# One channel tile of a depthwise convolution goes from TensorE to ScalarE and GpSimd

## What is computed

```
def mixer_conformer_conv(x, w_pw1, b_pw1, w_dw, b_dw, ln_g, ln_b, w_pw2):
    h = x @ w_pw1 + b_pw1
    a, g = jnp.split(h, 2, axis=-1)
    h = a * jax.nn.sigmoid(g)
    h = causal_depthwise_conv(h, w_dw) + b_dw          # 31 taps, each channel on its own
    h = jax.nn.silu(layer_norm(h, ln_g, ln_b))
    return h @ w_pw2
```

## Time and profile before

| | |
|---|---|
| median of 3 runs | 2520.3 us (2519.31 to 2522.27) |
| the profiled execution | 2518.05 us, its span 2516.3 us |
| TensorE busy | 2491.3 us, 99% |
| VectorE, ScalarE, GpSimd busy | 1921.5, 1124.3, 2.4 us |
| TensorE's granted clock | 1.0 of full speed over the span |
| TensorE's taps, layer 0 | from 100.3 to about 156.6 us |
| the same, layer 3 | from 1986.7 to about 2044.5 us |

### The profile page before, as it was taken

How to read it: one execution, slowest core, us unless ns; L and a number is a source line. 1 busy time by engine, 2 the same in 40 slices (tenths; PEclk the granted TensorE clock), 3 DMA queues, 4 the chain that set the end, 5 groups by cost and what they waited for, 6 DMA issues and landing times.

```text
span 2516.3 us, 43772 instructions
## 1 busy us (share of the span) xinstructions
PE 2491.3 (99%) x18687; PEld 2281.9 (91%) x18687; DVE 1921.5 (76%) x2564; ACT 1124.3 (45%) x1580; POOL 2.4 (0%) x15
## 2 busy tenths in 40 slices
PE   9999999999999999999999999999999999999999
PEld 7899999889888899998898899998898899999888
DVE  7779999578454689995784479997677779999576
ACT  4466444336233254443362245444353476444335
POOL 0000000000000000000000000000000000000000
PEclk9999999999999999999999999999999999999999
DMA  5203333323222223333233324333223203333322
GB/s 157 69 27 94 104 107 102 108 79 132 99 93 85 90 86 108 103 109 101 84 101 95 98 67 118 110 102 109 92 86 101 67 27 94 107 104 109 102 84 76
DMA packets 264502, 238.15 MB, mean 95 GB/s; under 512 B 14396, under 2 KB 210292, under 8 KB 264180
## 3 DMA queue, kind: packets, MB, share of 16 engines
q1 hardware_dynamic: 263732, 234.84, 30.0%
q10 hardware_dynamic: 576, 0.52, 0.1%
HBM read 233.21 MB, written 2.10 MB: 94 GB/s over the span
## 4 chain that ended last, share of the span: by engine, by line
PE 87%; DVE 4%; ACT 0%; issue 0%; DVEq 0%
PE psum L985 15%; PE psum L1150 10%; PE psum L1152 10%; PE psum L1151 9%; PE psum L853 9%; PE psum L854 9%; PE psum L855 9%; PE psum L871 3%; PE psum L873 3%; PE psum L872 3%; PE psum L843 2%; PE psum L844 2%; PE psum L849 2%; PE psum L914 2%; DVE w_lo L1687 1%; PE psum L1193 1%
## 5 line engine op out<-in xcount | busy, mean ns | idle before, releaser
L1687 DVE TENSOR_TENSOR w_lo<-raw,w_hi 128x1024 fp32r<-128x1024 f32 x287 | 345.3, 1222 | 255.2 <-ACT w_hi L1270 254.7
L1270 ACT CAST w_hi<-raw 128x1024 fp32r<-128x1024 f32 x287 | 295.2, 1046 | 403.7 <-DMA raw<-in_ffn_w_down_dram 101.1
L853 PE MATMUL psum<-h_hi,w_lo 128*128 128x512 f32 x872 | 341.5, 392 | 0.0
L855 PE MATMUL psum<-h_hi,w_hi 128*128 128x512 f32 x872 | 339.4, 389 | 0.0
L854 PE MATMUL psum<-h_lo,w_hi 128*128 128x512 f32 x856 | 333.2, 389 | 0.0
L985 PE MATMUL psum<-a_hi,w_lo 128*128 128x256 f32 x1088 | 275.3, 282 | 6.8 <-DVE w_lo L1687 3.8
L985 PE MATMUL psum<-a_hi,w_hi 128*128 128x256 f32 x1088 | 271.5, 279 | 0.0
L1152 PE MATMUL psum<-h_hi,w_hi 128*128 128x256 f32 x768 | 218.2, 284 | 0.0
L1151 PE MATMUL psum<-h_hi,w_hi 128*128 128x256 f32 x768 | 217.2, 283 | 0.0
L985 PEld LDWEIGHTS psum<-a_hi,w_lo 128*128 128x128 f32 x1088 | 204.4, 188 | 8.9 <-DVE w_lo L1687 3.4
L1282 ACT CAST w_hi<-w_hi_f 128x1024 fp32r<-128x1024 f32 x96 | 101.1, 1053 | 233.0 <-DVE w_hi_f L1715 233.0
(11 more groups left out here) (326 smaller groups left out, 6124.6 us busy)
## 6 DMA issues: line engine op xcount, KB each, us to landing
raw<-in_ffn_w_gate_dram SPq DMA_DIRECT2D x176, 256.0 KB, 3.0
raw<-in_ffn_w_up_dram SPq DMA_DIRECT2D x176, 256.0 KB, 3.4
raw<-in_ffn_w_down_dram SPq DMA_DIRECT2D x176, 256.0 KB, 3.0
raw<-in_a_w_pw_dram SPq DMA_DIRECT2D x94, 256.0 KB, 3.0
raw<-in_ple_w_gate_dram SPq DMA_DIRECT2D x64, 256.0 KB, 3.0
raw<-in_b_w_in_dram SPq DMA_DIRECT2D x64, 256.0 KB, 3.0
raw<-in_c_w_in_dram SPq DMA_DIRECT2D x48, 256.0 KB, 2.9
raw<-in_b_w_out_dram SPq DMA_DIRECT2D x32, 256.0 KB, 3.0
```

The costliest lines, as they stand in the source:

```text
L853: pe.matmul(bank(grp.g, j), st_lo, mv_hi, start=(k == 0), stop=False, skip_group_check=by_tiles(grp))
L855: done = pe.matmul(bank(grp.g, j), st_hi, mv_hi, start=False, stop=(ku == last and a == UK - 1), skip_group_check=by_tiles(grp))
L1270: act.copy(hi_u[u % RING], raw_u[u % RING]).then_inc(hi_ready, 1)
L1687: dve.tensor_tensor(lo_u[u % RING], raw_u[u % RING], hi_u[u % RING].bitcast(F32), ALU.subtract)\
```

## The change

Tile 2 leaves `QUADS`. ScalarE multiplies the shifted `conv_x` by the tap weight, once for each of the 31 taps, into a ring of five buffers of 512 words; GpSimd adds each product to the tile in `h_f32` where the moved segments also lie. ScalarE's products stand behind its weight casts of groups 2 and 3, four for each (`TAPS_UNIT`). Product k from the sixth on waits until the add that frees its buffer is done; each add waits for its product and for the add before it.

The segments are then tiles 3, 4, 5, 6 and the two halves of 7. The rough mean is asked for at step 29 of segment 1 instead of step 14 of segment 3. VectorE waits for the last add in front of `centre_sum`, sums tiles 0, 1 and 2, moves the low half of segment 0 itself and adds tile 3. Moves, centring, sums and squares are regrouped to match; the order of the last statements of the norm's first half changes a little on ScalarE and VectorE.

```diff
-QUADS = (2, 3, 4, 5, 6, 7)
-A_BLOCKS = 5
+POOL_TILE = 2
+PRODUCTS, TAPS_UNIT = 5, 4
+QUADS = (3, 4, 5, 6, 7)
+A_BLOCKS = 4
...
-SEGMENTS = ((0, None), (1, None), (2, None), (3, None), (4, None), (5, 0), (5, 1))
-WHOLE = 5
-CENTRE_IN, CENTRE_AT = 3, 14
+SEGMENTS = ((0, None), (1, None), (2, None), (3, None), (4, 0), (4, 1))
+CENTRE_IN, CENTRE_AT = 1, 29
...
+        def tap_product(k):
+
+            at = A_BLOCKS * BLOCK_WORDS + CW + k % PRODUCTS * SEQ
+            return a_f32[:, at:at + SEQ]
...
+            for s in stages:
+                if s.kind != "conv_in":
+                    continue
+                c, y = s.layer // 3, tiles(h_f32, CONV_Y + POOL_TILE)
+                for k in range(1, TAPS_A):
+                    pool.wait_ge(tap_made, TAPS_A * c + k + 1)
+                    if k > 1:
+                        pool.wait_ge(tap_added, (TAPS_A - 1) * c + k - 1)
+                    pool.tensor_tensor(y, tap_product(k - 1) if k == 1 else y, tap_product(k), ALU.add).then_inc(tap_added, 1)
...
+            def tap_products(s, first, end):
+
+                for k in range(first, min(end, TAPS_A)):
+                    if k >= PRODUCTS:
+                        act.wait_ge(tap_added, (TAPS_A - 1) * (s.layer // 3) + k - PRODUCTS + (k == PRODUCTS))
+                    act.activation(tap_product(k), conv_x[:, POOL_TILE, k:k + SEQ], ACT.Identity,
+                                   scale=col("a_w_dw", s.layer // 3 * TAPS_A + k, POOL_TILE)).then_inc(tap_made, 1)
...
                 half_moments(s, 0)
                 half_root(s, 0)
                 load_silu()
+                half_affine_pair(s, 0, 0)
                 move(s, LAST, 1)
-                half_affine_pair(s, 0, 0)
                 half_affine_pair(s, 0, 1)
...
+                        conv_by_phase(s, 3)
                         conv_by_phase(s, 4)
-                        conv_by_phase(s, 5)
                         split_more(AHEAD)
-                        for i in range(2):
-                            move(s, i, 1)
-                            move(s, i, 0)
-                        move(s, 2, 0)
+                        move(s, 0, 1)
                         save_centre(s)
+                        move(s, 1, 1)
+                        act.wait_ge(moved_low, moved(s, 0))
+                        move(s, 1, 0)
                         conv_squares(s)
-                        act.wait_ge(moved_high, moved(s, 2))
+                        conv_square(s, 4)
+                        move(s, 2, 1)
+                        conv_square(s, 5)
                         move(s, 3, 1)
...
                             split_to(u + 1)
+                            if grp.index == 2 and u == grp.unit + LEAD:
+                                act.wait_ge(prod_ready, s.prod0 + POOL_TILE // 2 + 1)
+                            if grp.index >= 2:
+                                made = (TILES * (grp.index - 2) + u - grp.unit - LEAD) * TAPS_UNIT
+                                tap_products(s, made, made + TAPS_UNIT)
...
             def centre_sum(s):
 
                 own.settle()
+                partial, bias = tiles(tmp, 4), lambda m: conv_bias(s, m)
+                dve.wait_ge(tap_added, (TAPS_A - 1) * (s.layer // 3 + 1))
+                own.add(dve.scalar_tensor_tensor(partial, conv_tile(2), bias(2), conv_tile(0), ALU.add, ALU.add))
+                own.settle()
+                own.add(dve.tensor_tensor(partial, partial, conv_tile(1), ALU.add))
+                move(s, 0, 0)
                 wait_moved(s, 0)
-                wait_moved(s, 1)
-                for m in range(2):
-                    own.add(dve.scalar_tensor_tensor(tiles(tmp, 4 + m), conv_tile(2 + m), conv_bias(s, 2 + m), conv_tile(m),
-                                                     ALU.add, ALU.add))
-                own.settle()
-                dve.tensor_tensor(ysum[:, :], tiles(tmp, 4), tiles(tmp, 5), ALU.add).then_inc(ysum_ready, 1)
+                own.settle()
+                dve.scalar_tensor_tensor(ysum[:, :], conv_tile(3), bias(3), partial, ALU.add, ALU.add).then_inc(ysum_ready, 1)
...
                         make_blocks(s, 4)
-                        make_blocks(s, 5)
                         lo_to(ahead)
```

More of the change, by code:

```diff
@@ L34 @@
 LAST = len(SEGMENTS) - 1
-Z_READY = 3 + len(SEGMENTS) - 2
-SQ_READY = len(SEGMENTS) - 1
+Z_READY = 4 + len(SEGMENTS) - 2
+SQ_READY = len(SEGMENTS)
 SGU_BLOCK = 128
@@ L375, in tap_blocks @@
             return h_f32[:, SPLIT_LOW:SPLIT_LOW + (TAPS_A + 2) * PAIR_ROWS]
+        def tap_product(k):
+            at = A_BLOCKS * BLOCK_WORDS + CW + k % PRODUCTS * SEQ
+            return a_f32[:, at:at + SEQ]
+        assert A_BLOCKS * BLOCK_WORDS + CW + PRODUCTS * SEQ <= 2 * DT * SEQ
         def rows(ap, r):
@@ L573, in trunk @@
         moved_low = sem("moved_low")
+        tap_made = sem("tap_made")
+        tap_added = sem("tap_added")
         proj_sq = sem("proj_sq")
@@ L1350, in conv_half_square @@
                 m, h = QUADS[SEGMENTS[i][0]], SEGMENTS[i][1]
-                act.wait_ge(z_ready, Z_READY * (s.layer // 3) + i + 2)
+                act.wait_ge(z_ready, Z_READY * (s.layer // 3) + i + 3)
                 act.activation(hcol(square(m), h), hcol(tiles(h_f32, CONV_Y + m), h), ACT.Square).then_inc(sq_ready, 1)
@@ L1660, in _ @@
                             split_to(u + 1)
+                            if grp.index == 2 and u == grp.unit + LEAD:
[3 more added lines that the diff above has]
+                                tap_products(s, made, made + TAPS_UNIT)
                             if u == s.groups[3].unit + s.groups[3].units + 1:
-                                for n in range(4):
+                                for n in range(3):
                                     conv_by_phase(s, n)
@@ L1841, in conv_sums_of @@
                 sum_sq, sum_z, both = tiles(tmp, 4), tiles(tmp, 5), tiles(tmp, 4, 2)
-                move(s, 2, 1)
                 dve.wait_ge(centre_saved, c + 1)
@@ L1847, in conv_sums_of @@
                 place_centred(s, 3)
-                wait_moved(s, 2)
-                place_centred(s, 4)
-                move(s, 3, 0)
                 dve.wait_ge(z_ready, z0 + 3)
@@ L1854, in conv_sums_of @@
                 own.add(dve.tensor_tensor(sum_z, sum_sq, sum_z, ALU.add))
-                wait_moved(s, 3)
-                place_centred(s, 5)
+                wait_moved(s, 1)
+                place_centred(s, 4)
+                dve.wait_ge(z_ready, z0 + 4)
+                own.settle()
+                own.add(dve.tensor_tensor(sum_z, sum_z, conv_tile(4), ALU.add))
+                move(s, 2, 0)
                 dve.wait_ge(sq_ready, SQ_READY * c + 1)
                 own.add(dve.tensor_tensor(tiles(tmp, 0, 2), tiles(tmp, 0, 2), tiles(tmp, 2, 2), ALU.add))
[L1859 to L1862, removed]
+                own.settle()
                 own.add(dve.tensor_tensor(sum_sq, tiles(tmp, 0), tiles(tmp, 1), ALU.add))
+                wait_moved(s, 2)
+                place_centred(s, 5)
+                dve.wait_ge(sq_ready, SQ_READY * c + 2)
+                own.settle()
+                own.add(dve.tensor_tensor(sum_sq, sum_sq, square(4), ALU.add))
                 dve.wait_ge(z_ready, z0 + 5)
-                own.settle(back=1)
                 own.add(dve.tensor_tensor(sum_z, sum_z, conv_tile(5), ALU.add))
[L1867 to L1870, removed]
+                move(s, 3, 0)
+                wait_moved(s, 3)
                 place_centred(s, 6)
@@ L1879, in conv_sums_of, with place_half @@
                 own.add(dve.tensor_tensor(sum_sq, sum_sq, square(6), ALU.add))
-            def move_half(s, i):
-                move(s, i, 0)
+            def place_half(s, i):
                 wait_moved(s, i)
@@ L1889, in add_half @@
                 c, m, h = s.layer // 3, QUADS[SEGMENTS[i][0]], SEGMENTS[i][1]
-                dve.wait_ge(z_ready, Z_READY * c + i + 2)
+                dve.wait_ge(z_ready, Z_READY * c + i + 3)
                 own.settle()
@@ L1897, in add_half_square @@
                 c, m, h = s.layer // 3, QUADS[SEGMENTS[i][0]], SEGMENTS[i][1]
-                dve.wait_ge(sq_ready, SQ_READY * c + i)
+                dve.wait_ge(sq_ready, SQ_READY * c + i + 1)
                 own.settle()
@@ L1903, in conv_norm @@
             def conv_norm(s):
-                move_half(s, 5)
-                add_half(s, 5)
-                add_half_square(s, 5)
+                move(s, LAST - 1, 0)
+                place_half(s, LAST - 1)
+                add_half(s, LAST - 1)
+                add_half_square(s, LAST - 1)
                 half_root(s, 0)
@@ L1910, in conv_norm @@
                 half_scale(s, 0, 1)
-                move_half(s, 6)
-                add_half(s, 6)
+                move(s, LAST, 0)
                 half_lo_pair(s, 0, 0)
                 half_scale(s, 0, 2)
+                place_half(s, LAST)
+                add_half(s, LAST)
                 half_lo_pair(s, 0, 1)
```

(2 more changed lines are left out.)

5 lines of the change are left out of this document (removed).

## The result

| | before | changed |
|---|---|---|
| median | 2519.8 us (4 runs) | 2554.1 us (4 runs) |
| the profiled execution / its span | 2518.05 / 2516.3 | 2553.88 / 2552.1 us |
| ratio | | 1.014 (95%: 1.0126 to 1.0155) |

The change makes the kernel 34 us slower, about 17 in each convolution layer. The forecast was 2559, in a case in which VectorE and GpSimd take turns.

A forecast was written before the change was run, and what follows sets the result against it. TensorE, busy 99%, was taken as the bound, with VectorE nearly full before the taps. Centre 28.2 us late less 8.6 gained gives 19.6 a layer: 2518 + 39 = 2557, 2559 on the median's scale; range 2500 to 2580.

The forecast's parts named there:

- What bounds the kernel: Whole kernel: TensorE busy 99% of the span; VectorE nearly full in the stage before layer 0's taps, 40.47 of 42.80 us.
- One quad leaves TensorE: Convolution taps: one whole segment of 34 steps goes, -7.72 us per layer.
- The end of the taps: Half segments before the norm's sums: VectorE's queue empties in time, removing TensorE's idle time, -0.87 us per layer.
- 31 products on ScalarE at 0: ScalarE before the taps: 31 products of 0.63 us, 19.5 us, fit beside 14.54 busy and add no term.
- The centre moved ahead: Rough mean in segment 1, due at 114.87: VectorE's queue ends at 114.73, leaving 0.14 us; some 0.7 in layer 3.
- What an add costs VectorE: VectorE before the centre: each GpSimd add costs it 1.02 us, 30.7 per layer; break-even at 0.37 an add.
- Turns: Main case: VectorE and GpSimd alternate on SBUF operands; 2559 us, own range 2537 to 2580, chance 0.56.
- The sum: Per convolution layer: centre 28.2 us late, less the gain of 8.6, makes 19.6 us longer, 39 in two.
- Clean: Rival: adds run beside VectorE without touching it, only the 17.2 us gain remains; 2503 us, chance 0.30.
- Long adds alone: Rival: chained adds exceed 1.63 us each and end late without holding VectorE; 2524 us, chance 0.04.
- A late ScalarE: Rival: products' waits hold ScalarE's weight casts, a sigmoid 6 us late; no term of its own, no separate chance.
- Slight interference: Rival: up to some 0.5 us an add, GpSimd touching memory only part of its time; 2503 to 2525, chance 0.10.

The follow-up runs named there:

- the narrow adds: Changed kernel with 29 of a layer's 30 GpSimd adds one column wide instead of 512, all waits and products kept; 2498.8 us, ratio 0.9923.
- the two kernels with ten adds: Kernel before plus ten spare 128x512 GpSimd adds, started by the last gated input (2518.5 us) or by VectorE's sum for the centre (2520.1 us).
- Thirty adds in the old order: Kernel before plus 30 chained spare GpSimd adds from the second gated input, VectorE waiting for them before its centre sum; 2566.1 us, ratio 1.0189.
- The copies: Changed kernel with each GpSimd add replaced by a copy of the product into the tile, one operand read; 2515.9 us, ratio 0.9993.
- 12 taps: Kernel before with the last 12 of tile 2's 31 taps moved from TensorE to VectorE's idle time before the centre sum; 2513.0 us, ratio 0.9979.

## Why the prediction was right, point by point

- **What bounds the kernel.** Right: VectorE, 95% busy in the stage, was the engine to watch. Shown by the narrow adds (VectorE free, 2498.8 us) and by the changed kernel (TensorE waits for VectorE at six places in layer 0, up to the centre).
- **One quad leaves TensorE, -7.72.** Right; 272 instructions less a layer. With the two terms below it makes 19.4 us when nothing holds VectorE.
- **The end of the taps, -0.87.** Right, but a term was missing. In front of the second product TensorE stood idle 1.36 us for the first tiles of the norm (157.95, shown with the narrow adds). In the changed kernel ScalarE makes these before it moves the last half segment; TensorE, in the kernel with narrow adds, goes from the last tap to that product (149.19) with no gap that the trace lists. 7.72 + 0.87 + 1.36 = 9.95 a layer, 19.9 in two, against 19.4 measured. The prediction gave this exchange of two lines no price. That the exchange is what removes the gap is argued: it was not tried alone.
- **31 products on ScalarE at 0.** Right: narrow adds leave them all in and lose nothing. One takes 0.73 us by itself, and four in a row 2.57, 0.64 each, against the 0.63 of the sum.
- **The centre moved ahead, with 0.14 us left.** Right: with narrow adds it comes without idle time in front of it, and VectorE's sum is ready at 114.51 + 0.75, 0.4 us before L915 starts. The "some 0.7 us" of layer 3 doesn't come out of the rows cited: 1996.90 - 1.25 + 5.39 = 2001.04 against 1986.65 + 14.53 = 2001.18 is 0.14 again. It takes in a pause of 0.61 us that TensorE makes in its first segment there, at 1991.77, and that the text doesn't name.
- **What an add costs VectorE.** Turns, as forecast. An add that meets an instruction with two operands in SBUF costs 1.01 to 1.08 us by the rows of four kernels (changed kernel 1.03 and 1.04, the one wide add 1.05, the two kernels with ten adds 1.08 and 1.01), and the average over all adds is 1.00 by VectorE's busy time, where the forecast had 1.1 and 1.02. That the size came out so well is partly luck: it was an add length of 1.1, held in full, times 0.93. Alone, adds are 1.36 apart, and a third of a microsecond of that holds nobody; the two errors cancel. The Trainium skill, SBUF — State Buffer, section Who interferes with whom, says that VectorE's instructions with two inputs in SBUF contend with GpSimd instructions that read SBUF and not with those that only write; the trace agrees on all three kinds (two operands 1.03 us, one 0.35, memset 0; copies from PSUM untouched). That the second comer is held for the whole of the first, as the prediction cites it, goes too far here: two adds alone last 2.63 us and start 1.36 apart, so one lasts about 1.27 us, and VectorE is held 1.03 of it.
- **The sum.** Centre late by 28.2: measured 142.12 against 114.87, and 0.36 on top, as the stage began that much earlier, 27.6. One term more was missing, the clock: TensorE ran the segments behind the centre at a granted 0.91, 18.34 us from the centre to the first half segment (160.46). The kernel with narrow adds, at 1.00, takes 17.65 for the same (115.69 to 133.34), so the clock adds 0.7. 27.6 + 0.7 - 9.95 = 18.4; the first matmul of the second product is 18.7 late in layer 0 (176.32 + 0.36 against 157.95). In layer 3 it is 17.0: the changed kernel needs the same 57.3 us there from its first tap to this matmul, but the kernel before took 59.2 us instead of 57.6, with more short pauses in its segments. So a forecast of 19.6 a layer stands against 17 to 19 measured.
- **Chances.** Clean would have been 2499, as the narrow adds show. Long adds alone: no, VectorE comes to its wait for the last add 18.8 us after that add's end. A late ScalarE: no, VectorE had nothing to wait for in the stage (the windows below list it busy 22.79 of 22.90, 15.00 of 15.00 and 14.97 of 15.00 us). Slight interference: no, though a one-operand GpSimd instruction would have been that case. Its upper end was added up wrongly: 30 x 0.5 - 11.07 = 3.9 a layer makes 2528 by the median's scale, not 2525.
- **Expectations that failed.** Thirty adds in the old order: 47 us against 27. I counted VectorE's idle time at the centre as cover for work queued ahead of it, where only the 6.35 us lead of a remainder covered anything. In the changed kernel the same waits on the dense product occur, but there the centre has no slack and VectorE's queue decides anyway. The copies: 2515.9 against 2534, as said there.

## What to carry to other kernels

Before work goes to GpSimd, list what VectorE does meanwhile: if it reads two operands from SBUF, an add on GpSimd costs VectorE more (1.03 us here) than the same step would cost if VectorE did it itself (0.68 to 0.78). In these runs adds were free for VectorE only where it was idle or read one of its operands from PSUM; VectorE instructions with a single operand in SBUF and none in PSUM were not tried beside adds. Slack at one wait is cover only for work that stands behind every earlier deadline of the same queue; 12 taps put there gained 5.9 us, while 30 adds put in front of it lost 47.

## What the runs showed of the hardware

What GpSimd reads, at 128x512 in float32, sets what a VectorE instruction with both operands in SBUF loses beside it: about 1.03 us for an add, about 0.35 for a copy, nothing for a memset (0.53 us long) or for adds of one column. VectorE's copies from PSUM (3.20 us for eight) and its gated inputs, with one operand in PSUM (1.40), are untouched.

TensorE's clock falls behind short stops. Windows of the changed kernel in layer 0 (busy us of TensorE, weight loads, VectorE, ScalarE, GpSimd, then the granted clock):

```profile
57.10:80.00 22.90, 21.07 (x93) 17.10 (x92) 22.79 (x16) 16.09 (x24) 18.31 (x12) 1.00 0.32 99
80.00:95.00 15.00, 9.45 (x29) 7.31 (x30) 15.00 (x10) 8.26 (x11) 13.85 (x9) 0.80 0.19 60
95.00:110.00 15.00, 12.29 (x44) 9.23 (x43) 14.97 (x16) 8.50 (x11) 10.12 (x7) 0.86 0.11 36
...
142.00:158.00 16.00, 15.88 (x495) 15.78 (x499) 10.76 (x17) 12.23 (x27) 0.00 (x0) 0.89 0.01 4
158.00:175.00 17.00, 17.00 (x333) 16.38 (x326) 12.40 (x25) 9.32 (x20) 0.00 (x0) 1.00 0.01 3
```

It is at 1.00 up to 80, and below it in the windows behind the stops of 2.44 and 4.93 us; the matmul behind the second stop takes 0.79 us where 0.39 is normal, the lower of the two levels (1.2 instead of 2.4 GHz). After the stop of 3.65 us at the centre it is below full again, and back at 1.00 from 158 on. Where TensorE has to wait for VectorE anyway this is hidden; behind the last wait it costs, 0.7 us a layer here, and 1.8 in the kernel before with 30 adds.
